# Two pairs of modulation weights move from the GpSimd queue into the weight ring of the SyncE queue

## The chip, the cores and the metric

The kernel runs on one core of a Trainium2 chip (trn2). The metric is the device time of one execution in microseconds (us), as the median of several runs. All data is float32; each large product is made from float32 weights that ScalarE and VectorE split into a high and a low part.

## The reference, cut to what matters

One decoder layer, for 256 prompt tokens and 8 sample tokens together (264 columns). Each of its three blocks begins with an RMS norm that is shifted and scaled by rows of a modulation matrix `mod`, which is itself a product of the conditioning vectors with `w_ada`:

```
mod = silu(c) @ w_ada + b_ada                      # 1024 x 9216, nine rows of 1024
x = x + 0.5 * g1 * SwiGLU_1(rmsnorm(x)*(1+sc1) + sh1)
h = rmsnorm(x)*(1+sc2) + sh2
q, k, v (both branches), gates = h @ w_in          # projections
out_a, out_b = attention over own tokens and paged K/V caches
x = x + g2 * ((sig(gA) * yA + sig(gB) * yB) @ w_out)
x = x + 0.5 * g3 * SwiGLU_2(rmsnorm(x)*(1+sc3) + sh3)
```

## The kernel before

**Stages.** Each engine has one instruction stream, written by hand, and the engines wait for one another on semaphores. In order: a prologue; the first feed-forward block (11 pairs of gate and up weights, then 12 blocks of down weights, `W_DN1` to `W_DN1 + 11`); the projections (`W_QK` to `W_QK + 3` for q, `W_KV` and the seven after it for k and v, then the gates) with the sample tokens' cache blocks scored beside them; attention; the output product; the second feed-forward block.

**The weight ring.** A weight block is 1 MB (or 0.75 MB) and lands in one of four buffers `raw` (`raw_50` to `raw_53` in the listings below are slots 0 to 3). SyncE (SP) issues the loads in the order of `stream_plan`, and `slots` gives each the slot that was filled longest ago. Before a load SP waits in `slot_free` (line 486) until the slot's former content is used up: for a weight block this is its second low half (semaphore `lo_ready`, written by VectorE, DVE), for a pair of modulation weights the product on TensorE (PE) that reads it (semaphore `ada_multiplied`). ScalarE (ACT) copies each half of a landed block to `whi` (`hi`, line 661), DVE subtracts to get `wlo` (`lo`, line 963), PE then runs three products for each chunk (`product`, line 1428). SP works in order, so whatever stands behind a waiting load waits too.

**Modulation weights.** `w_ada` is cut into sets of 2048 columns; a set `sc` has eight 1 MB pieces of 128 rows, which PE reads in four pairs, `ada(sc, q, key_c)` (line 1460). Sets 0 to 2 come through `early` buffers and the ring. Set 3 (`ada(3, 0)` to `ada(3, 3)`, lines 1572 to 1576, after the down blocks and around the sum for the norm) is read from eight `held_ada` buffers, which GpSimd (POOL) loads through its own DMA queue (lines 593 to 598): two when the last gate and up product is done, six when the last activation has been split.

**Around the q projection.** After the last down product: DVE updates `x` (line 1045), ACT squares and takes the root (lines 676, 681), DVE inverts (line 989), then DVE and ACT make the normed input chunk by chunk (lines 998, 700, 1016), on which PE starts `W_QK`. ACT then works through `hi` of `W_QK + 1` (both halves) and `W_QK + 2` (first half) and so on, one block ahead of PE, with the heads' roots (`head_root`, line 683) between; DVE likewise with `lo`, `head_reciprocal` (line 1119) and `head_norm` (line 1123), then it turns the first cache blocks (`turn_keys`, line 1147, L1152 in the rows). SP and POOL each load two cache blocks (`kvA` and `kvB`, eight transfers of 256 KB each) as soon as the last down product is done; POOL loads a third, `kvB_lent`, when the normed input is complete (semaphore `hlo_ready`). SP's `kvA` loads stand behind the loads of `W_QK` to `W_KV` in its order.

A piece of `w_in`, `w_down`, gate or up is fetched in rows of 1 KB (256 columns), a piece of `w_ada` and a cache page in rows of 8 KB.

Of the kernel before, what the change touches and what calls it, by code (L numbers as in the profile page):

```python
# [39 lines left out]
UNIT = 2048  # L40
# [8 lines left out]
W_FF1, W_DN1 = 0, 22  # L49
W_QK, W_KV, W_GATE, W_BR, W_OUT = 34, 38, 46, 54, 58  # L50
# [8 lines left out]
def stream_plan():  # L59
    plan = []  # L60
    ada = lambda c: [("ada", c, 0), ("ada", c, 1)]
    for c in range(ADA_RING):
        plan += ada(c)
    for i in range(NPAIR):
        plan += [("w", W_FF1 + 2 * i)] + (ada(ADA_PRO + i) if i < FF_ADA else []) + [("w", W_FF1 + 2 * i + 1)]
    plan += [("w", W_DN1 + u) for u in range(12)] + [("w", n) for n in range(W_QK, W_DN2 + 12)]
    return plan


# [138 lines left out]
def build(nc, A, O):  # L208
    ctx = ExitStack()
    with ctx:  # L210
# [11 lines left out]
        def sem(name):  # L222
            return ctx.enter_context(nc.semaphore(name))
# [33 lines left out]
        yst = place("yst", [P, 2, D], where=r)  # L257
        ysts = place("ysts", [TS, D], where=r)

        held_at = [hhi_at, hlo_at] + [sil_at + 4 * UNIT * e for e in range(6)]  # L260
        held_ada = [place(f"held_ada{e}", [P, UNIT], where=[o]) for e, o in enumerate(held_at)]

        r = [region]
# [61 lines left out]

        s_raw = [sem(f"raw_landed{s}") for s in range(SLOTS)]
        s_early = [sem(f"early_ada_landed{h}") for h in range(2 * (ADA_PRO - ADA_RING))]
        s_held, s_last = [sem(f"held_ada_landed{e}") for e in range(8)], [sem(f"last_ada_landed{e}") for e in range(4)]
        s_rows, s_crow, s_x, s_const = sem("rows_landed"), sem("crow_landed"), sem("x_landed"), sem("const_landed")
        s_const_late, s_ptab = sem("late_const_landed"), sem("page_table_landed")  # L330
        s_hi, s_lo, s_gemm = sem("hi_ready"), sem("lo_ready"), sem("gemm_done")
# [153 lines left out]
        def _(sp):  # L485
# [52 lines left out]
            sp.wait_ge(s_ptab, 16)  # L538
            for u in range(12):
                load_w(W_DN1 + u)  # L540
            for u in range(4):
                load_w(W_QK + u)
            load_w(W_KV)
            sp.wait_ge(s_gemm, half_done(W_QK - 1, 1))
# [41 lines left out]
        @block.gpsimd  # L586
        def _(pool):
            late = CW["dist"][0]
            pool.dma_start(const[:, 0:late], A["consts"][:, 0:late]).then_inc(s_const, 16)

            pool.wait_ge(s_sil, 1)
            pool.dma_start(const[:, late:NCONST], A["consts"][:, late:NCONST]).then_inc(s_const_late, 16)
            pool.wait_ge(s_gemm, half_done(W_DN1 - 1, 1))
            for e in range(2):
                pool.dma_start(held_ada[e][:, :], ada_src(3, e)).then_inc(s_held[e], 16)
            pool.wait_ge(s_alo, NPAIR)
            for e in range(2, 8):
                pool.dma_start(held_ada[e][:, :], ada_src(3, e)).then_inc(s_held[e], 16)
            pool.wait_ge(s_gemm, half_done(W_QK - 1, 1))
            pool.wait_ge(s_ptab, 16)  # L600
            for use in range(KVS):
                kv_load(pool, 1, use)

            def row_out(name, ab, p, src, srcs, done):
                c0 = 256 * p
                name += ("_moba", "_diff")[ab]
                dst = O[name + "_prompt"][0, 0].rearrange("(a p) h d -> p a (h d)", p=P)[:, :, c0:c0 + 256]
                dsts = O[name + "_sample"][0, :, 0].rearrange("s h d -> s (h d)")[:, c0:c0 + 256]
                f0 = 512 * ab + c0
                pool.dma_start(dst, src[:, :, f0:f0 + 256]).then_inc(done, 16)  # L610
                pool.dma_start(dsts, srcs[:, f0:f0 + 256]).then_inc(done, 16)

            K_ROWS = {6: 0, 10: 1, 12: 2, 14: 3}
            V_ROWS = {7: 0, 15: 1, 17: 2, 19: 3}
            pool.wait_ge(s_ada, ADA_N2 + 4)
            for b in range(2):
                ins = nc.gpsimd.memset(qrow[b][:, :, :], 0.0)
            ins.then_inc(s_qzero, 1)
            def lo(n, t):

                key = ("w", n)
                s = slot_of(key)
                pool.wait_ge(s_raw[s], landed(key))
                pool.wait_ge(s_hi, half_done(n, t))
                pool.wait_ge(s_lo, half_done(n, t) - 1)
                nc.gpsimd.tensor_tensor(half_view(wlo[n % 2], key, t), half_view(raw[s], key, t), half_view(whi[n % 2], key, t).bitcast(F32),  # L626
                                        ALU.subtract).then_inc(s_lo, 1)

            for use in range(KVS, 4 * TS):
                kv_load(pool, 1, use)  # L630
                if use + 2 < POOL_HALVES:
                    lo(*filler(use + 2))
                if use in K_ROWS:
                    i = K_ROWS[use]
                    pool.wait_ge(s_tok, 4 * (i + 1))
                    row_out("k", i // 2, i % 2, ktok, ktoks, s_krow)
                if use in V_ROWS:
                    i = V_ROWS[use]
                    pool.wait_ge(s_vtok, 4 * (i + 1))
                    row_out("v", i // 2, i % 2, vtok, vtoks, s_vrow)  # L640

            def load_last(e):
                pool.dma_start(ada_dst(last_ada[e], ADAS - 1), ada_src(ADAS - 1, e)).then_inc(s_last[e], 16)

            pool.wait_ge(s_pv, 4 * TS)
            load_last(0)
            pool.wait_ge(s_vrow, 16 * 8)
            pool.wait_ge(s_po, KC)
            load_last(1)
            pool.wait_ge(s_ext, 2)  # L650
            load_last(2)
            load_last(3)
# [772 lines left out]
        def _(pe):  # L1425
# [34 lines left out]
            def ada(sc, q, key_c):  # L1460

                b = 4 + sc % 2
                narrow = sc == ADAS - 1
                if q == 0 and sc >= 2:
                    pe.wait_ge(s_adaT, sc - 1)
                for half in range(2):
                    if key_c is None:
                        e = 2 * (q - (ADA_RING if sc == 0 else 0)) + half
                        landing, buf = ((s_early, early) if sc == 0 else (s_last, last_ada) if narrow else (s_held, held_ada))
                        pe.wait_ge(landing[e], 16)  # L1470
                        w = buf[e]
                    else:
                        key = ("ada", key_c, half)
                        s = slot_of(key)
                        pe.wait_ge(s_raw[s], landed(key))
                        w = raw[s]
                    u = 2 * q + half
                    for k in range(2 if narrow else 1):
                        kc = 2 * u + k if narrow else u
                        rows_ = w[:, 1024 * k:1024 * k + 1024] if narrow else w[:, :]  # L1480
                        cols = rows_.rearrange("p (t j a) -> p t j a", j=4, a=32)
                        n = 256 if narrow else 512
                        for j in range(4):
                            ins = mm(bank[32 * j:32 * j + 32, b, 0:n].rearrange("p (t a) -> p t a", a=32), csilu[:, kc, :], cols[:, :, j, :],  # L1484
                                     start=(kc == 0), stop=(kc == KC - 1))
                ins.then_inc(s_ada, 1)
# [63 lines left out]
            def down(first, pairs, alos, xups, with_ada):  # L1550
                for cb in range(4):
                    for third in range(3):
                        n = first + 3 * cb + third
                        if cb == 0:
                            pe.wait_ge(s_alo, alos - NPAIR + (4, 8, 11)[third])
                        if third == 0:
                            if cb == 0:
                                pe.wait_ge(s_sil, pairs)
                            elif cb == 1:
                                pe.wait_ge(s_act, pairs)  # L1560
                            else:
                                pe.wait_ge(s_xup, xups + cb - 1)
                        nk = min(FC - 8 * third, 8)
                        for t in range(2):
                            block_half(2 * (cb % 2), n, n % 2, t, ahi, alo, nk=nk, k0=8 * third, first=(third == 0), last=(third == 2))
                        u = 3 * cb + third
                        if with_ada and cb and third == 1:
                            norm_sum(1, cb - 1)
                        if not with_ada and cb and third == 1:
                            y_turn(cb - 1)  # L1570
                if with_ada:
                    ada(3, 0, None)
                    norm_sum(1, 3)
                    ada(3, 1, None)
                    ada(3, 2, None)
                    ada(3, 3, None)
                else:
                    y_turn(3)

# [345 lines left out]
```

## Time and profile before

| | us |
|---|---|
| median of 3 runs | 784.88 |
| lowest and highest | 783.54 to 786.91 |
| the profiled execution | 784.88 |
| its span in the profile | 783.2 |

Busy shares of the span are PE 93%, DVE 61%, ACT 41%, POOL 16%. The mean DMA rate is 268 GB/s. The profiled execution took 784.88 us, 1.7 us more than the span, and is also the median run, so that a change of the span can be added to the median directly. In the views below a time is counted from the span's start. "SPq" and "POOLq" are the issuing parts of SP and POOL. A group "x3" is three instructions in a row; its length runs from the first start to the last end.

### The profile page before, as it was taken

To read this page: it belongs to the slowest core of one execution; us is meant where nothing else is said; L and a number is where in the kernel's file an instruction comes from. 1 tells how busy PE (TensorE), PEld (TensorE's weight loads), DVE (VectorE), ACT (ScalarE), POOL (GpSimd) and SP (SyncE) were. 2 spreads that over 40 slices of the span, in tenths; PEclk is the share of its full clock that TensorE was granted. 3 is DMA by queue.
4 is the path that set the end of the run, shared out by engine and by line. 5 is a ranking of instruction groups with operands and counts; after the bars stand their busy time and mean duration, and the time that the engine had idled before them with its cause. 6 is when DMAs were issued, how large, how long until landed. Compare 5 with 4: busy or idle time off the path is not lost.

```text
span 783.2 us, 16961 instructions
## 1 busy us (share of the span) xinstructions
PE 730.3 (93%) x6610; PEld 647.7 (83%) x6610; DVE 479.3 (61%) x684; ACT 320.3 (41%) x515; POOL 123.8 (16%) x179
## 2 busy tenths in 40 slices
PE   5589999999999998988878999999989999999997
PEld 2369889999999797877765666669979999999997
DVE  1635454555454899999987554677766465454551
ACT  1434333344242653333314544364445444444331
POOL 0000000002000402877863332210000000000000
PEclk9799999999999999999978999999999999999999
DMA  9979898867986764999999999995625655646530
GB/s 352 381 254 344 291 321 302 269 195 267 395 277 210 273 213 142 388 400 407 405 391 342 404 403 348 342 364 191 199 72 164 205 168 171 204 148 201 165 105 28
DMA packets 116520, 209.53 MB, mean 268 GB/s; under 512 B 6714, under 2 KB 100186, under 8 KB 104162
## 3 DMA queue, kind: packets, MB, share of 16 engines
q1 hardware_dynamic: 106784, 159.47, 59.1%
q0 software_dynamic: 9440, 49.02, 16.0%
q8 instruction: 46, 0.75, 0.4%
q14 instruction: 24, 0.20, 0.1%
q10 hardware_dynamic: 226, 0.10, 0.1%
HBM read 205.31 MB, written 3.24 MB: 266 GB/s over the span
## 4 chain that ended last, share of the span: by engine, by line
PE 70%; DVE 18%; DMA 6%; issue 2%; ACT 2%; SPq 1%; ACTq 0%; DVEq 0%
PE bank L1433 19%; PE bank L1434 19%; PE bank L1435 19%; DMA early<-in_w_ada 3%; PE bank L1789 3%; DVE kvB L1152 2%; DVE kvA L1152 2%; PE bank L1484 2%; DMA kvA<-in_cache_k_moba 2%; DVE rstd L1132 2%; PE bank L1749 1%; DVE wlo L969 1%; DMA raw<-in_w_ada 1%; DVE kvB_lent L1152 1%; PE bank L1750 1%
## 5 line engine op out<-in xcount | busy, mean ns | idle before, releaser
L969 DVE TENSOR_TENSOR wlo<-raw,whi 128x1024 fp32r<-128x1024 f32 (+1 forms) x177 | 208.6, 1199 | 190.3 <-ACT whi L671 187.6
L1433 PE MATMUL bank<-hhi,whi 128*128 128x264 f32 x992 | 288.6, 291 | 11.4 <-DVE wlo L969 7.5
L1434 PE MATMUL bank<-hlo,whi 128*128 128x264 f32 x992 | 283.5, 286 | 0.0
L1435 PE MATMUL bank<-hhi,wlo 128*128 128x264 f32 x992 | 283.1, 285 | 0.0
L671 ACT ACTIVATE whi<-raw 128x1024 fp32r<-128x1024 f32 (+1 forms) x192 | 194.5, 1034 | 119.6 <-PE bank L1435 83.1
L1433 PEld LDWEIGHTS bank<-hhi,whi 128*128 128x128 f32 x992 | 189.3, 191 | 24.6 <-issue 15.1
L1434 PEld LDWEIGHTS bank<-hlo,whi 128*128 128x128 f32 x992 | 189.3, 191 | 0.2
L1435 PEld LDWEIGHTS bank<-hhi,wlo 128*128 128x128 f32 x992 | 188.4, 190 | 0.0
L1433 PE MATMUL bank<-ahi,whi 128*128 128x264 f32 x416 | 119.6, 288 | 0.4 <-DVE alo L1391 0.4
L1435 PE MATMUL bank<-ahi,wlo 128*128 128x264 f32 x416 | 118.1, 284 | 0.0
L1434 PE MATMUL bank<-alo,whi 128*128 128x264 f32 x416 | 117.8, 283 | 0.0
L1433 PEld LDWEIGHTS bank<-ahi,whi 128*128 128x128 f32 x416 | 78.2, 188 | 0.9 <-DVE alo L1391 0.6
L1434 PEld LDWEIGHTS bank<-alo,whi 128*128 128x128 f32 x416 | 78.3, 188 | 0.2
L1435 PEld LDWEIGHTS bank<-ahi,wlo 128*128 128x128 f32 x416 | 78.3, 188 | 0.0
L443 POOL DMA_DIRECT2D kvB<-in_cache_k_diff x44 | 23.2, 528 | 112.1 <-issue 64.8
L706 ACT ACTIVATE sil<-bank 128x528 f32<-128x528 f32 x22 | 13.4, 611 | 62.9 <-PE bank L1435 62.9
L710 ACT ACTIVATE ahi<-act 128x528 f32 (+1 forms) x22 | 14.2, 646 | 54.2 <-DVE act L1023 54.2
L626 POOL TENSOR_TENSOR wlo<-raw,whi 128x1024 fp32r<-128x1024 f32 x15 | 35.9, 2392 | 2.8 <-issue 2.5
L443 POOL DMA_DIRECT2D kvB<-in_cache_v_diff x44 | 23.2, 528 | 51.0 <-PE bank L1789 41.9
L1749 PE MATMUL bank<-hhi,whi 128*128 128x264 f32 x96 | 28.5, 297 | 0.0
L1027 DVE TENSOR_TENSOR alo<-act,ahi 128x528 f32 (+1 forms) x22 | 15.6, 709 | 19.1 <-ACT ahi L710 19.1
L1750 PE MATMUL bank<-hlo,whi 128*128 128x264 f32 x96 | 27.3, 284 | 0.0
(246 smaller groups left out, 804.9 us busy)
## 6 DMA issues: line engine op xcount, KB each, us to landing
raw<-in_ffn_w_gate SPq DMA_DIRECT2D x22, 1024.0 KB, 5.4
raw<-in_ffn_w_up SPq DMA_DIRECT2D x22, 1024.0 KB, 5.4
raw<-in_w_ada SPq DMA_DIRECT2D x20, 1024.0 KB, 8.3
raw<-in_w_in SPq DMA_DIRECT2D x20, 1024.0 KB, 10.5
raw<-in_ffn_w_down SPq DMA_DIRECT2D x16, 1024.0 KB, 5.3
kvB<-in_cache_k_diff POOLq DMA_DIRECT2D x44, 256.0 KB, 6.4
kvA<-in_cache_k_moba SPq DMA_DIRECT2D x44, 256.0 KB, 8.0
kvA<-in_cache_v_moba SPq DMA_DIRECT2D x44, 256.0 KB, 6.3
```

Source lines behind the costliest of these rows:

```text
L443: eng.dma_start(rows_, cache[bass.ds(page, 1)].rearrange("a (j t) d -> (a j) (t d)", t=4)).then_inc(s_kv[ab][use % KVS], 16)
L626: nc.gpsimd.tensor_tensor(half_view(wlo[n % 2], key, t), half_view(raw[s], key, t), half_view(whi[n % 2], key, t).bitcast(F32), ALU.subtra ...
L671: nc.scalar.activation(half_view(whi[key[1] % 2], key, t), half_view(raw[s], key, t), ACT.Copy).then_inc(s_hi, 1)
L969: dve.tensor_tensor(half_view(wlo[key[1] % 2], key, t), half_view(raw[s], key, t), half_view(whi[key[1] % 2], key, t).bitcast(F32), ALU.su ...
L1132: dve.reciprocal(rstd[:, i % 2, :], rstd[:, i % 2, :]).then_inc(s_krecip, 1)
L1152: dve.transpose(slot, slot).then_inc(s_kT[ab], 1)
L1433: mm(out, wh, xh, start=start, stop=False)
L1434: mm(out, wh, xl, start=False, stop=False)
L1435: return mm(out, wl, xh, start=False, stop=stop)
L1749: mm(out, wh, hhi[:, k, :], start=(k == 0), stop=False)
L1750: mm(out, wh, hlo[:, k, :], start=False, stop=False)
L1789: ins = mm(bank[32 * q:32 * q + 32, 4 + ab, :], wpad[half][:, q, ab, w0:w0 + 32], kv_slot(ab, use)[:, q, :], start=(half == 0 and c % 4 == ...
```

## The change

Of set 3 only the first four pieces are still loaded by POOL into `held_ada`. The last two pairs (`ADA_N2 + 2` and `ADA_N2 + 3`, four pieces of 1 MB) go through the ring on SP's queue, between `W_QK` and `W_QK + 1`. `ada(3, 2)` and `ada(3, 3)` read them from there. `W_QK + 1`, `W_QK + 2`, `W_QK + 3` and `W_KV` thereby follow in slots that these pairs hold. POOL's wait for all of set 3 ahead of zeroing `qrow` goes, since the buffers that overlapped it are gone.

```diff
@@ stream_plan
-    plan += [("w", W_DN1 + u) for u in range(12)] + [("w", n) for n in range(W_QK, W_DN2 + 12)]
+    plan += [("w", W_DN1 + u) for u in range(12)] + [("w", W_QK)] + ada(ADA_N2 + 2) + ada(ADA_N2 + 3)
+    plan += [("w", n) for n in range(W_QK + 1, W_DN2 + 12)]
@@ buffers and semaphores
-        held_at = [hhi_at, hlo_at] + [sil_at + 4 * UNIT * e for e in range(6)]
+        held_at = [hhi_at, hlo_at, sil_at, sil_at + 4 * UNIT]
-        s_held, s_last = [sem(f"held_ada_landed{e}") for e in range(8)], [sem(f"last_ada_landed{e}") for e in range(4)]
+        s_held, s_last = [sem(f"held_ada_landed{e}") for e in range(4)], [sem(f"last_ada_landed{e}") for e in range(4)]
@@ sync
             for u in range(12):
                 load_w(W_DN1 + u)
-            for u in range(4):
+            load_w(W_QK)
+            load_pair(ADA_N2 + 2)
+            load_pair(ADA_N2 + 3)
+
+            for u in range(1, 4):
                 load_w(W_QK + u)
             load_w(W_KV)
@@ gpsimd
-            for e in range(2, 8):
+            for e in range(2, 4):
                 pool.dma_start(held_ada[e][:, :], ada_src(3, e)).then_inc(s_held[e], 16)
...
-            pool.wait_ge(s_ada, ADA_N2 + 4)
             for b in range(2):
                 ins = nc.gpsimd.memset(qrow[b][:, :, :], 0.0)
@@ tensor
-                    ada(3, 2, None)
-                    ada(3, 3, None)
+                    ada(3, 2, ADA_N2 + 2)
+                    ada(3, 3, ADA_N2 + 3)
```

SP's order around the end of the first feed-forward block, from its last down block to its first cache page, in the kernel before. The brackets are the semaphores that the instruction waits for.

```order
L508 DMA raw_51<-in_ffn_w_down 128x6x256 [waits lo_ready]
L508 DMA raw_52<-in_w_in 128x8x256 [waits lo_ready]
L508 DMA raw_53<-in_w_in 128x8x256 [waits lo_ready]
L508 DMA raw_50<-in_w_in 128x8x256 [waits lo_ready]
L508 DMA raw_51<-in_w_in 128x8x256 [waits lo_ready]
L508 DMA raw_52<-in_w_in 128x8x256 [waits lo_ready]
L434 TENSOR_LOAD ptab [waits gemm_done]
```

The same place in the changed kernel (its line numbers are one higher).

```order
L509 DMA raw_51<-in_ffn_w_down 128x6x256 [waits lo_ready]
L509 DMA raw_52<-in_w_in 128x8x256 [waits lo_ready]
L503 DMA raw_53<-in_w_ada 128x2048 [waits lo_ready]
L503 DMA raw_50<-in_w_ada 128x2048 [waits lo_ready]
L503 DMA raw_51<-in_w_ada 128x2048 [waits lo_ready]
L503 DMA raw_52<-in_w_ada 128x2048 [waits lo_ready]
L509 DMA raw_53<-in_w_in 128x8x256 [waits ada_multiplied]
L509 DMA raw_50<-in_w_in 128x8x256 [waits ada_multiplied]
L509 DMA raw_51<-in_w_in 128x8x256 [waits ada_multiplied]
L509 DMA raw_52<-in_w_in 128x8x256 [waits ada_multiplied]
L435 TENSOR_LOAD ptab [waits gemm_done]
```

The four `w_in` loads `W_QK + 1` to `W_KV` stood behind waits on DVE's work in the down stage; they now stand behind waits on PE's modulation products, which come after that stage, and everything behind them on SP moves with them.

POOL's order in the kernel before, from the first piece of set 3 on; `held_ada_77` to `held_ada_84` are its eight buffers.

```order
L595 DMA held_ada_77<-in_w_ada 128x2048
L595 DMA held_ada_78<-in_w_ada 128x2048
L598 DMA held_ada_79<-in_w_ada 128x2048
L598 DMA held_ada_80<-in_w_ada 128x2048
L598 DMA held_ada_81<-in_w_ada 128x2048
L598 DMA held_ada_82<-in_w_ada 128x2048
```

Two more pieces follow it. The same place on POOL in the changed kernel, to its first read of the page table.

```order
L600 DMA held_ada_77<-in_w_ada 128x2048
L600 DMA held_ada_78<-in_w_ada 128x2048
L603 DMA held_ada_79<-in_w_ada 128x2048
L603 DMA held_ada_80<-in_w_ada 128x2048
L435 TENSOR_LOAD ptab
```

POOL issues four pieces instead of eight. The orders of PE, ACT and DVE stay as they are.

## Rows read from the trace of the kernel before

**Rows 1.** Chain of waits, 186 to 253 us: shares by line.
```profile
by line: PE bank L1435 32.2%; PE bank L1433 32.0%; PE bank L1434 31.8%; PE bank L1492 4.0%; issue 0.0%
```

**Rows 2.** Chain of waits, 268 to 400 us: start, length, what (us).
```profile
286.14 1.23 DVE wlo L969
287.37 3.38 DVE rstd L1121
...
291.54 2.22 DVE kvA L1152
...
377.90 1.08 PE bank L1678 x32
```

**Rows 3.** VectorE alone: stretch, length, busy time (instructions), clock, DMA share, GB/s.
```profile
266.90:286.10 19.20, 18.55 (x14) 1.00 0.73 241
286.10:377.90 91.80, 89.71 (x90) 1.00 0.86 326
```

**Rows 4.** Timeline, TensorE's modulation products: start, length, line, tile, count.
```profile
44.96 1.92 PE L1484 MATMUL bank<-raw,csilu 128*32 128x512 f32 x16
...
252.89 1.92 PE L1484 MATMUL bank<-held_ada,csilu 128*32 128x512 f32 x16
...
255.99 5.36 PE L1484 MATMUL bank<-held_ada,csilu 128*32 128x512 f32 x48
```

**Rows 5.** Timeline, SyncE's issues, same columns.
```profile
46.94 0.82 SPq L502 DMA_DIRECT2D raw<-in_w_ada  x2
...
49.53 4.01 SPq L513 DMA_DIRECT2D raw<-in_ffn_w_gate  x1
...
227.01 23.58 SPq L508 DMA_DIRECT2D raw<-in_w_in  x5
256.41 5.82 SPq L443 DMA_DIRECT2D kvA<-in_cache_k_moba  x8
272.64 7.06 SPq L508 DMA_DIRECT2D raw<-in_w_in  x2
```

**Rows 6.** Timeline, GpSimd's issues; in brackets the idle time before and its releaser.
```profile
256.35 4.55 POOL L443 DMA_DIRECT2D kvB<-in_cache_k_diff  x8 [64.45 <-issue]
267.20 2.25 POOL L443 DMA_DIRECT2D kvB_lent<-in_cache_k_diff  x4 [6.30 <-DVE hlo L1016]
```

**Rows 7.** L508's two w_in loads issued 243.9 and 250.2: time to landing.
```profile
DMA to landing us min/median/max: 5.0/5.1/5.1
```

**Rows 8.** One line's loads: the w_down load issued at 190.0.
```profile
L508 SPq DMA_DIRECT2D raw<-in_ffn_w_down x1: 368/368/368, 190.0 to 190.0; - x1
...
DMA to landing us min/median/max: 20.9/20.9/20.9
```

**Rows 9.** DMA queues, 189 to 211 us; q0 is GpSimd's, q1 SyncE's.
```profile
q0 software_dynamic: 1107, 8.15, 89.9%
q1 hardware_dynamic: 861, 0.86, 11.3%
```

**Rows 10.** All engines by stretch: the last three figures are clock, DMA share, GB/s.
```profile
190.00:210.00 20.00, 20.00 (x168) 20.00 (x167) 8.20 (x13) 5.20 (x6) 1.89 (x4) 1.00 1.02 411
213.00:227.00 14.00, 14.00 (x115) 13.87 (x113) 8.55 (x11) 6.46 (x8) 0.00 (x0) 1.00 1.10 348
```

**Rows 11.** DMA traffic, 258 to 273 us.
```profile
DMA packets 947, 5.15 MB, mean 343 GB/s; under 512 B 320, under 2 KB 320, under 8 KB 320
```

**Rows 12.** Timeline of ScalarE around the q projection.
```profile
265.86 2.94 ACT L671 ACTIVATE whi<-raw 128x1024 fp32r<-128x1024 f32 x3
...
271.61 1.06 ACT L671 ACTIVATE whi<-raw 128x1024 fp32r<-128x1024 f32 x1 [0.88 <-PE bank L1435]
```

**Rows 13.** Timeline of VectorE around the q projection.
```profile
272.78 1.22 DVE L969 TENSOR_TENSOR wlo<-raw,whi 128x1024 fp32r<-128x1024 f32 x1 [0.17 <-ACT whi L671]
273.92 3.44 DVE L1121 RECIPROCAL rstd<-rstd 128x528 f32<-128x528 f32 x1
```

**Rows 14.** Waits, 180 to 255 us: who waited for whom; total, times, longest.
```profile
ACT whi L671 <- DMA raw<-in_ffn_w_down: 3.8, 2, 2.8
```

## The prediction, made before the changed kernel had run

> **What bounds the kernel now.** I read the chain of waits first, then the stages around the changed loads, then the queues.
>
> In the down stage the chain runs through TensorE alone, nearly all of it weight products [rows 1]: no load and no other engine sets the time there. From 286 us to 378 us it runs through VectorE: low halves, head norms, turning of cache blocks, and it goes back to TensorE only at 377.9 [rows 2]. VectorE alone shows how full it is: 89.7 of 91.8 us, and already 18.55 of 19.2 us in the stretch before, 266.9 to 286.1 [rows 3]. So TensorE's 93% doesn't say what a delay in the q projection is worth. VectorE has 0.65 us to spare from 267 to 286 and what it loses beyond that is paid to the end, because everything it does afterwards stands in its fixed order.
>
> **What goes.** POOL's eight pieces become four. In the stretch in which they are in flight POOL's queue moves 8.15 MB and SP's 0.86 MB [rows 9], and a down block issued then lands after 20.9 us [rows 8]. That will get better by about 4 MB, some 10 us of DMA time at 411 GB/s [rows 10]. It is worth nothing: the chain in that stage has no load and no VectorE row in it [rows 1], so TensorE's work hides it. For POOL's removed wait I take nothing too: TensorE ends set 3 at 261.35 (255.99 + 5.36) [rows 4], and POOL zeroes `qrow` only behind the issue of kvB_lent at 267.2 to 269.45 [rows 6], so the wait was over long before.
>
> **What the new pieces need.** SP now issues them where it issued `W_QK + 1` to `W_KV`, the last at about 250.2, and such a load lands 5.1 us later [rows 5, 7]: 255.3. TensorE reads the last piece in the last eighth of a group that ends at 261.35, about 260.7. Five microseconds to spare: nothing.
>
> **What is moved.** The loads of `W_QK + 1`, `+ 2`, `+ 3` and `W_KV` wait for `ada(3, 2)` (the first two) and `ada(3, 3)`. The group of 48 products is three such steps of 1.79 us, so `ada(3, 2)` ends at 259.6 and `ada(3, 3)` at 261.35 [rows 4]. How fast SP follows is seen early in the kernel: products end at 46.88 (44.96 + 1.92), the next pair's load is issued at 46.94 [rows 4, 5]. So `W_QK + 1` is issued at 259.7 instead of some 233. The question is whether it and the next two still land when they are needed.
>
> Need: ScalarE starts on `W_QK + 1` at 265.86, and on the first half of `W_QK + 3` at 271.61 [rows 12]. VectorE makes that half's low part at 272.78 and then begins the first head reciprocal at 273.92 [rows 13].
>
> Supply. Back to back, 1 KB rows move at 348 GB/s, 8 KB rows at 411 [rows 10]: 1.05 MB takes 3.0 us and 2.55 us. An undisturbed load lands after 5.1 us [rows 7], so about 2.1 us of it is not transfer. When POOL's queue has 8 KB rows in flight, SP's 1 KB rows get 0.86 of 9.01 MB, a tenth [rows 9]. And POOL does have such rows in flight: kvB's 2.1 MB from 256.35 on, kvB_lent's 1.05 MB from 267.2 on [rows 6]. Before, the loads beside them were kvA's, with rows of 8 KB too, and nothing was late.
> - kvB: bytes from 256.35 + 2.1 = 258.45, 5.1 us at 411 GB/s, over at 263.5.
> - `W_QK + 1`: bytes from 259.7 + 2.1 = 261.8; a tenth of the rate until 263.5 (0.07 MB), then 0.98 MB in 2.8 us: 266.3. That is 0.45 us after 265.86.
> - `W_QK + 2`: 3.0 us more, 269.3.
> - kvB_lent: bytes from 269.3 on, 2.6 us to 271.9. `W_QK + 3` gets 0.1 MB in that time, the other 0.95 MB need 2.7 us: 274.6. `W_KV`: 277.6.
>
> So ScalarE can start on `W_QK + 3` at 274.6; its copy takes 1.06 us and VectorE's step 1.22 us [rows 12, 13], with 0.1 us between: VectorE is at the reciprocal at 277.0 instead of 273.92, **3.1 us late**. Of its 0.65 us of spare time [rows 3] about half lies behind this point, 0.3 us. 2.8 us remain. TensorE itself is hardly held: `W_QK + 1` starts some 0.5 us later, and `W_QK + 3` is due there only at about 282. The delay goes through VectorE to the reciprocals and cache blocks of the chain [rows 2].
>
> kvA moves too. SP's last `w_in` issue may be held until the queue drains (such an issue took 4.0 us with three loads in front [rows 5]), so to about 266; then the page table (kvA's first issue at 256.41 came 3.5 us after the end of the down stage at 252.9), then 5.8 us for eight issues [rows 4, 5]: `W_KV + 1` is issued at 275.3 instead of 272.64. Bytes in order: `W_KV` until 277.6, kvA 5.1 us until 282.7, `W_KV + 1` until 285.7. Its low half was made at 286.14 [rows 2], now at 288.9, so it has to land by 287.8: 2.1 us to spare. kvA is first turned at 291.54 [rows 2]; 282.7 is early enough.
>
> Sum: -0 (POOL's burst) + 0 (new pieces) + 2.8 (VectorE through `W_QK + 3`) + 0 (kvA, `W_KV + 1`). Against the profiled execution: span 783.2 + 2.8 = 786.0, plus the 1.7 us outside it, **787.7**; the profiled execution is the median.
>
> **Bounds.** Lower: if SP's queue were served as though alone, three loads from 261.8 end at 270.8, before 271.61: nothing lost, 784.9. Below nothing I see no term, since no wait on the chain goes. Upper: all bytes of POOL first and the mixed rate of 343 GB/s [rows 11]: 3.15 MB of weights, 0.7 MB of kvB left at 261.8, 1.05 MB of kvB_lent, 4.9 MB in 14.3 us: 276.1, 4.5 us late, 4.2 after the spare time: 789.1. I take 2.8, from the shares of rows 9 and the full rates of rows 10, as they are for the same two row sizes.
>
> **A rule beside the rows.** [Rows 8] show a 1 MB load that took 20.9 us. The Trainium skill, DMA: Bandwidth & Descriptors, section "Anatomy of one DMA — SWDGE (gpsimd) path", fits a transfer as 2.0 us plus bytes over 436 GB/s. By that alone, an estimate, `W_QK + 1` would land at 259.7 + 4.4 = 264.1, the third load at about 269, and nothing would be late (784.9, the first rival's result). The same page, section "Queues, rings and completion order", has each DMA engine take turns between queues packet by packet, without regard to bytes; rows 9, with 8.15 against 0.86 MB at rows of 8 against 1 KB, agree with turns by count.
>
> **The rivals.**
> - *The loads come in time* (784.9). The condition: kvB and kvB_lent take less from SP's queue than a tenth-to-nine-tenths split, or end sooner, so that `W_QK + 3` has landed by 272. For: kvB is only 2 MB where rows 9 had 8, and POOL issues it in pieces of 256 KB that may leave gaps (the mean rate there was 343, not 411 GB/s [rows 11]). Against: the bytes have to pass in any order, and 4.9 MB take 11.9 us even at 411 GB/s, so not before 273.7 unless kvB_lent falls behind.
> - *A second load is late as well* (slower). The issue of `W_QK + 3` and `W_KV` is held longer than 4 us and takes the page table, kvA and `W_KV + 1` with it; POOL's next transfers share with them. From a landing of 287.8 on each microsecond counts. For: behind a queue slowed to a tenth an issue should be held longer than 4.0 us. Against: there are 2.1 us to spare, and what waits in the queue is transferred meanwhile. If the held issue takes twice as long and ends at 270, `W_KV + 1` is issued at 279.3 and lands at about 290: 2.2 us more, 789.9.
> - *The freed burst is worth something* (faster). ScalarE does wait 3.8 us for down blocks in that stage [rows 14]; if TensorE waited with it, all of that would come back: 784.9 - 3.8 = 781.1. Against it, [rows 1] have no such wait in the chain, TensorE being a block behind.
>
> **How the numbers follow.** Forecast (1 to 4.2 us lost): 0.57. In time: 0.2. Second load late: 0.18. Faster: 0.03; the rest is what I don't see. The time is the forecast's, 787.7. The range goes from 784.0 (in time, with the spread of the runs before) to 790.5 (the second load late). A measurement of this kernel can tell about 0.5%, 3.9 us, from no change: faster than 781.0 is 0.04; slower than 788.8 takes most of the second rival and the upper end of the forecast, 0.26; within, 0.70.
>
> **What would show it.** Right, step by step: no change of TensorE's time up to 252.9; `w_in` loads issued at about 259.7, 260.1, 261.4; landings after 6.6 us and then about 9 and 13 us instead of 5.1; a wait of ScalarE on a `w_in` load of some 2 us shortly before 275, and VectorE's first wide reciprocal near 277; the chain from there on as before, about 3 us later, up to the end. Wrong: a first reciprocal still at 274 (the loads came in time), a VectorE wait before 289 on `W_KV + 1` (second rival), a down stage that ends before 252.5, or a delay at 290 that has gone by 400.

## The result: 5.6 us slower, and where they went

The changed kernel takes **790.42 us** (median of 7 runs, 788.2 to 792.2), the kernel before 784.78 us (783.39 to 786.91, 7 runs beside them). The ratio is 1.0076, 95% interval 1.0053 to 1.0097. The ratios here and below are not the quotients of the printed medians, from which they differ by up to 0.002. The forecast was 787.7: slower, by half of what was measured.

The page of the profile of the changed kernel (span 789.4 us) answers to the shares given in the section on the time before. Total busy times have hardly moved (TensorE 733.2 us after, 730.3 before in the page); what was added is waiting.

```profile
span 789.4 us, 16961 instructions
PE 733.2 (93%) x6610; PEld 651.9 (83%) x6610; DVE 480.1 (61%) x684; ACT 320.8 (41%) x515; POOL 121.6 (15%) x175
```

The two profiled executions differ by 1.1 us before the change can matter (the prologue). I therefore count from VectorE's update of `x` at the end of the down stage, 253.00 us in the kernel before, 251.90 in the changed one; this point is called the mark below. First the timeline of the issues, SyncE's and then GpSimd's (start, length, count), to be held against [rows 5, 6].

```profile
232.20 17.24 SPq L503 DMA_DIRECT2D raw<-in_w_ada  x4
258.58 9.77 SPq L509 DMA_DIRECT2D raw<-in_w_in  x4
271.83 6.65 SPq L444 DMA_DIRECT2D kvA<-in_cache_k_moba  x8
278.52 6.37 SPq L509 DMA_DIRECT2D raw<-in_w_in  x2
...
255.24 4.55 POOL L444 DMA_DIRECT2D kvB<-in_cache_k_diff  x8 [66.53 <-issue]
266.09 2.25 POOL L444 DMA_DIRECT2D kvB_lent<-in_cache_k_diff  x4 [6.30 <-DVE hlo L1020]
```

`W_QK + 1` is issued at 258.58, 6.7 us after the mark, where the forecast put it (259.7 less 253.0). Now ScalarE and VectorE in the timeline of the changed kernel, to be held against [rows 12, 13]. The brackets are idle time and its releaser.

```profile
268.33 2.00 ACT L675 ACTIVATE whi<-raw 128x1024 fp32r<-128x1024 f32 x2 [3.48 <-DMA raw<-in_w_in]
272.57 1.06 ACT L675 ACTIVATE whi<-raw 128x1024 fp32r<-128x1024 f32 x1 [2.24 <-DMA raw<-in_w_in]
276.80 1.06 ACT L675 ACTIVATE whi<-raw 128x1024 fp32r<-128x1024 f32 x1 [1.23 <-DMA raw<-in_w_in]
...
269.49 1.23 DVE L973 TENSOR_TENSOR wlo<-raw,whi 128x1024 fp32r<-128x1024 f32 x1 [4.05 <-ACT whi L675]
277.96 1.23 DVE L973 TENSOR_TENSOR wlo<-raw,whi 128x1024 fp32r<-128x1024 f32 x1 [1.06 <-ACT whi L675]
279.11 3.45 DVE L1125 RECIPROCAL rstd<-rstd 128x528 f32<-128x528 f32 x1
285.65 3.45 DVE L1125 RECIPROCAL rstd<-rstd 128x528 f32<-128x528 f32 x1
```

ScalarE waits for three loads in a row: it stood ready for 3.5, 2.2 and 1.2 us when they landed. The first wide reciprocal stands 27.2 us after the mark; before it was 20.9 (273.92 less 253.00). That is 6.3 us, and the second one is 6.15 us late. The chain of waits of the changed kernel shows the same hand-over. It runs through the first late load, then TensorE, and from 290 on through VectorE as in [rows 2], each step some 6.2 us later after the mark.

```profile
253.10 0.65 ACT work L680
258.58 9.73 DMA raw<-in_w_in
268.33 1.07 ACT whi L675
269.49 1.24 DVE wlo L973
...
290.03 1.07 ACT whi L675
291.19 1.23 DVE wlo L973
292.42 3.37 DVE rstd L1125
295.81 0.77 DVE qT L1131
296.58 2.22 DVE kvA L1156
```

### The profile page after: what moved, and what is told of

The parts are those of the page before. It is cut to its first block, busy times and chain, and to the rows that moved or that the text cites. A ratio compares the mean times of both kernels' runs of the same rounds, so it can differ in the third digit from the quotient of the medians.

```text
span 789.4 us, 16961 instructions
## 1 busy us (share of the span) xinstructions
PE 733.2 (93%) x6610; PEld 651.9 (83%) x6610; DVE 480.1 (61%) x684; ACT 320.8 (41%) x515; POOL 121.6 (15%) x175
## 4 chain that ended last, share of the span: by engine, by line
PE 72%; DVE 13%; DMA 9%; issue 2%; ACT 2%; SPq 1%; ACTq 0%; DVEq 0%
PE bank L1437 19%; PE bank L1438 19%; PE bank L1439 19%; DMA early<-in_w_ada 3%; PE bank L1793 3%; PE bank L1488 2%; DMA kvA<-in_cache_k_moba 2%; DMA kvA_lent<-in_cache_k_moba 2%; DVE kvA L1156 2%; DVE kvB L1156 1%; PE bank L1753 1%; DMA raw<-in_w_in 1%; PE bank L1682 1%; DVE wlo L973 1%; PE bank L1754 1%
## 5 line engine op out<-in xcount | busy, mean ns | idle before, releaser
L710 ACT ACTIVATE sil<-bank 128x528 f32<-128x528 f32 x22 | 13.4, 611 | 61.6 <-PE bank L1439 61.6
L1754 PE MATMUL bank<-hlo,whi 128*128 128x264 f32 x96 | 27.2, 284 | 0.0
```

The costliest lines, as they stand in the source:

```text
L1754: mm(out, wh, hlo[:, k, :], start=False, stop=False)
```

## The experiments

For each run two positions on VectorE after the mark are given beside the time, read from the one profiled execution: the first wide reciprocal, and the second turned block of `kvA` (at 307.50 in the kernel before, 54.50 after the mark), by which the delay that is kept can be read. Kernels that differ only elsewhere agree in them within 0.1 us, where times scatter by 3. All ratios are to runs of the kernel before beside them.

| kernel | first reciprocal after the mark | against before | second `kvA` block against before | ratio of times (95%) |
|---|---|---|---|---|
| before | 20.92 | | | |
| changed | 27.21 | +6.29 | +6.16 | 1.0076 (1.0053 to 1.0097) |
| x1_wait_only | 27.65 | +6.73 | +6.39 | 1.0056 (1.0035 to 1.0077) |
| x2_kvb_later | 20.96 | +0.04 | +5.61 | 1.0080 (1.0053 to 1.0107) |
| x3_one_pair | 20.94 | +0.02 | +0.02 | 0.9989 (0.9969 to 1.0008) |
| x4_filler | 26.79 | +5.87 | +5.39 | 1.0083 (1.0053 to 1.0113) |
| x5_burst_spread | 20.92 | 0.00 | 0.00 | 0.9986 (0.9963 to 1.0009) |
| x6_kvb_after_kv1 | 20.91 | -0.01 | +1.34 | 1.0016 (0.9995 to 1.0038) |
| x7_lent_after_kv1 | 25.31 | +4.39 | +4.40 | 1.0061 (1.0038 to 1.0084) |
| x8_lent_filler | 23.91 | +2.99 | +2.57 | 1.0059 (1.0032 to 1.0087) |
| v1_pool_lo | 20.91 | -0.01 | -1.11 | 0.9970 (0.9946 to 0.9994) |
| v1_again | 20.91 | -0.01 | -1.11 | 0.9980 (0.9961 to 0.9999) |

The position of the `kvA` block is the one to hold against the times: on 785 us the ratios say 6.0 us for the changed kernel, 6.3 for x2 and 1.3 for x6. It differs from the first reciprocal's where a delay or a gain enters behind the reciprocal (x2, x6, v1) or where a delay is partly made up (x1, x4, x8). It lies within the ratio's interval in each run but x1, where it is 0.3 us above.

### x1_wait_only: the late issue alone, on the kernel before

```diff
-            for u in range(4):
-                load_w(W_QK + u)
+            load_w(W_QK)
+            sp.wait_ge(s_ada, ADA_N2 + 3)
+            load_w(W_QK + 1)
+            load_w(W_QK + 2)
+            sp.wait_ge(s_ada, ADA_N2 + 4)
+            load_w(W_QK + 3)
             load_w(W_KV)
```

> The kernel before with one thing from the change: SP waits for ada(3, 2) ahead of the load of W_QK + 1, and for ada(3, 3) ahead of W_QK + 3. The pieces of set 3 stay where they were, all eight on POOL's queue. Theory (the late issue of these loads is the whole loss): 788.5 to 792 us, like the changed kernel's 790.4, and VectorE's first wide reciprocal 5 to 6.5 us later than in the kernel before. Rival (the loss comes from reading or loading the pairs through the ring, or from POOL's shorter queue): below 786.5.

Measured: 790.86 us (787.67 to 792.91), reciprocal 6.7 us late, a little beyond the 6.5 expected. Two waits on SyncE make the whole loss without a single piece of set 3 in the ring. So the pairs in the ring and POOL's shorter queue are not needed for the loss. The timeline of VectorE, with the waits behind late copies:

```profile
270.04 1.23 DVE L973 TENSOR_TENSOR wlo<-raw,whi 128x1024 fp32r<-128x1024 f32 x1 [4.35 <-ACT whi L675]
275.53 1.23 DVE L973 TENSOR_TENSOR wlo<-raw,whi 128x1024 fp32r<-128x1024 f32 x1 [2.16 <-ACT whi L675]
279.79 3.45 DVE L1125 RECIPROCAL rstd<-rstd 128x528 f32<-128x528 f32 x1
```

### x3_one_pair: half the change

```diff
-    ... [("w", n) for n in range(W_QK, W_DN2 + 12)]
+    ... [("w", W_QK)] + ada(ADA_N2 + 3)
+    plan += [("w", n) for n in range(W_QK + 1, W_DN2 + 12)]
-            for e in range(2, 8):
+            for e in range(2, 6):
-                    ada(3, 3, None)
+                    ada(3, 3, ADA_N2 + 3)
```

(`held_at` and `s_held` get six entries, SP loads the one pair behind `W_QK`, POOL keeps its wait.)

> Half the change: only the last pair of set 3 goes through the ring, the other six pieces stay with POOL. By the slots W_QK + 1 and W_QK + 2 then keep their early issue (about 239 and 250), only W_QK + 3 and W_KV wait for ada(3, 3), to about 260 or 261. Theory (lateness of W_QK + 1 to + 3 against their use): W_QK + 3 lands 268 to 271, before it is needed at about 271.6, time 784 to 786. Rival (each piece in the ring costs, the dose halves the effect): 787 to 788.

Measured: 784.31 us (783.01 to 787.74), beside 785.19 of the kernel before; reciprocal in place. Half the dose costs nothing. `W_QK + 3` is issued at 260.5, as late as in the change, and lands after 7.4 us, at 267.9, before it is needed: `W_QK + 1` and `+ 2` are no longer in flight ahead of it. This is lateness against a use, not a cost per piece.

### x2_kvb_later: POOL silent beside the first three loads

```diff
             pool.wait_ge(s_ptab, 16)
+            pool.wait_ge(s_raw[slot_of(("w", W_QK + 3))], landed(("w", W_QK + 3)))
             for use in range(KVS):
                 kv_load(pool, 1, use)
```

> The changed kernel, but POOL issues its first three cache blocks only when W_QK + 3 has landed, so nothing of POOL's queue is in flight beside W_QK + 1 to W_QK + 3. Theory A (the loads lose their time to POOL's 8 KB rows): W_QK + 1 lands about 7 us after its issue as in the early pair issued at 46.94 (instead of 9.7), W_QK + 3 some 5 us earlier than in the changed kernel, time 785.5 to 787.5. Theory B (the issue at 259 is too late whatever stands beside it): W_QK + 3 earlier by less than 2 us, time 789 to 791. Both expect the first wide reciprocal to move with the landing of W_QK + 3.

Measured: 791.11 us (788.49 to 795.89), and the reciprocal back in its place. The loads issued at 258.6, 259.1 and 260.4 landed after 5.2, 7.8 and 9.6 us, in the changed kernel after 9.7, 13.5 and 16.5. So theory A holds for the landings, and B is out: issued as late as in the change, they come in time when POOL is silent. Yet nothing was won. A's range for the time was missed by 3.6 us, and the time lies at the upper edge of B's, whose mechanism is out. The timeline of VectorE and the landing of `W_KV + 1` in this kernel say why.

```profile
290.70 1.23 DVE L974 TENSOR_TENSOR wlo<-raw,whi 128x1024 fp32r<-128x1024 f32 x1 [5.71 <-ACT whi L676]
...
L509 SPq DMA_DIRECT2D raw<-in_w_in x1: 584/584/584, 272.7 to 272.7; - x1
...
DMA to landing us min/median/max: 16.8/16.8/16.8
```

kvB, now issued at 273.37, lies beside the next load that VectorE needs, and that one takes 16.8 us. The delay was moved from `W_QK + 3` to `W_KV + 1`: 5.6 us at the second `kvA` block. The first reciprocal alone would not have shown it.

### x6_kvb_after_kv1: POOL silent two loads longer

The same wait as in x2, on `("w", W_KV + 1)` instead of `("w", W_QK + 3)`.

> The changed kernel, but POOL issues its first three cache blocks only when W_KV + 1 has landed, two loads later than in x2_kvb_later. Theory A, amended (1 KB loads starve beside POOL's 8 KB rows wherever POOL is put, and in x2 it was W_KV + 1, landed after 16.8 us, that took over from W_QK + 3): W_KV + 1 lands by 281, the low half that stood at 286.14 stays within 1 us, kvB lands before its use at about 293, time 784.5 to 786.5. Rival (the change costs in some other way that x2 and the changed kernel share, the loads being a symptom): 789 to 791.

Measured: 786.99 us (785.03 to 788.96), 0.5 us above the expected range; ratio 1.0016, about 1.3 us, not told apart from none (by the medians it is 2.5). `W_KV + 1` landed after 9.3 us, at 282.7, and the low half that stood at 286.14 is in its place. In the trace the changed issue order with POOL's transfers out of the way loses 1.3 us instead of 6.2; by the times at least half of the loss is gone. What is left is seen in the timeline of VectorE: it waits 1.24 us for kvB, which now comes too late itself.

```profile
273.36 3.45 DVE L1126 RECIPROCAL rstd<-rstd 128x528 f32<-128x528 f32 x1
...
294.43 2.31 DVE L1157 STREAM_TRANSPOSE kvB<-kvB 128x2048 f32<-128x2048 f32 x1 [1.24 <-DMA kvB<-in_cache_k_diff]
```

### x7_lent_after_kv1: only the third cache block held back

```diff
             for use in range(KVS):
+                if use == KVS - 1:
+                    pool.wait_ge(s_raw[slot_of(("w", W_KV + 1))], landed(("w", W_KV + 1)))
                 kv_load(pool, 1, use)
```

> The changed kernel with only the third cache block (kvB_lent) held back until W_KV + 1 has landed; the first two as in the change. Theory A: kvB still makes W_QK + 1 and W_QK + 2 late, kvB_lent no longer W_QK + 3, which lands about 3 us earlier than in the changed kernel; first wide reciprocal about 3 us earlier, time 786.5 to 788.5. Rival (kvB alone makes all the delay, through the first landing): 789.5 to 791.

Measured: 790.72 us (787.73 to 794.12), reciprocal 4.4 us late instead of 6.3. The third load landed 13.4 us after its issue (16.5 in the change), 3.1 us earlier, as expected, but only 1.9 us arrived at the reciprocal. So with kvB alone beside the loads 4.4 us of delay are left. The expected 3 us at the reciprocal and the range of the time were missed; the time lies in the rival's range, though the trace doesn't bear the rival out, since 1.9 us did go. Something else stood right behind the landing. In the timeline of x7 VectorE waits for ScalarE's fourth copy, and that copy for TensorE:

```profile
276.01 1.06 ACT L677 ACTIVATE whi<-raw 128x1024 fp32r<-128x1024 f32 x1 [1.30 <-PE bank L1441]
277.17 1.23 DVE L975 TENSOR_TENSOR wlo<-raw,whi 128x1024 fp32r<-128x1024 f32 x1 [1.14 <-ACT whi L677]
278.31 3.45 DVE L1127 RECIPROCAL rstd<-rstd 128x528 f32<-128x528 f32 x1
```

### x4_filler and x8_lent_filler: TensorE's clock

In the changed kernel TensorE idles 4.38 us for `W_QK + 1`'s low half, and then its granted clock is at half (1.2 of 2.4 GHz). By stretch, with the clock as the third figure from the right:

```profile
265.00:269.50 4.50, 1.48 (x12) 1.27 (x11) 0.45 (x2) 1.17 (x2) 3.22 (x6) 1.00 1.09 352
269.70:276.50 6.80, 5.64 (x25) 5.67 (x26) 5.13 (x6) 3.64 (x5) 0.50 (x1) 0.50 1.06 375
```

Both kernels add work to TensorE in that idle time, x4 to the changed kernel and x8 to x7:

```diff
                     pe.wait_ge(s_xup, 4)
+                if u == 1:
+                    for c in range(KC):
+                        mm(bank[:, 7, 0:T], C("ones"), x[:, c, :], start=(c == 0), stop=(c == KC - 1))
```

> The changed kernel with eight added products on TensorE (ones by x into bank 7, not used for anything) between W_QK and W_QK + 1, about 3.6 us of work in TensorE's new idle time of 4 us. Theory C (part of the loss is TensorE's half clock from 269.7 to 276.5, which follows that idle time): no such stretch, W_QK + 1's products in 3 us a half instead of 6, and 2 to 3 us gained at the end: 787.5 to 788.5. Theory D (VectorE, behind the landing of W_QK + 3, sets the delay and TensorE's clock there is hidden): the clock stays up, but the reciprocal and the time stay, 789.5 to 791.

> x7_lent_after_kv1 with the eight added products of x4_filler on TensorE between W_QK and W_QK + 1. In x7 the landing of W_QK + 3 no longer held ScalarE; it waited 1.3 us for TensorE instead, whose clock had dropped to 1.2 GHz at 271.9 to 275.3. Theory (two delays lie side by side: the landings, and TensorE's clock after its idle time; with the first reduced the second sets the time): no such stretch and a first wide reciprocal 0.8 to 1.5 us earlier than in x7, time 0.5 to 1.5 us below x7. Rival (the clock is hidden here too, as in x4): the reciprocal within 0.3 us of x7's.

Measured: x4 791.43 us (789.96 to 794.05), reciprocal 26.79 after the mark, 0.4 us earlier than in the change. x8 790.26 us (785.43 to 792.95), reciprocal at 23.91, 1.4 us earlier than in x7. In both the low clock of 270 to 276 is gone. So both delays existed side by side. In x4 the landing of `W_QK + 3` is the later one, and ScalarE still waits for it; its own 0.4 us earlier landing is the whole 0.4 us at the reciprocal (theory D, and the time is 0.4 us above D's range). In x7 that landing is 21.8 after the mark and TensorE comes 1.2 us behind it; in x8 the landing is at 21.6 and sets the reciprocal again. Further on the clock counts for more: at the second `kvA` block x4 is 0.8 us ahead of the change and x8 1.8 us ahead of x7. In the times neither can be told: x8 is 0.5 us below x7, inside the scatter of both. From here, x8's timeline of VectorE:

```profile
276.02 2.38 DVE L975 TENSOR_TENSOR wlo<-raw,whi 128x1024 fp32r<-128x1024 f32 x2 [0.50 <-ACT whi L677]
278.32 3.45 DVE L1127 RECIPROCAL rstd<-rstd 128x528 f32<-128x528 f32 x1
```

(its mark is at 254.41, so 278.32 is 23.91 after it).

### x5_burst_spread: the shorter burst alone, on the kernel before

```diff
             for e in range(2, 8):
+                if e == 4:
+                    pool.wait_ge(s_gemm, half_done(W_DN1 + 5, 1))
                 pool.dma_start(held_ada[e][:, :], ada_src(3, e)).then_inc(s_held[e], 16)
```

> The kernel before, with POOL's burst halved alone: the last four pieces of set 3 are issued only after the sixth down block, everything else unchanged. If the shorter burst is worth something by itself, 781 to 783.5; if TensorE hides it, as the forecast has it, within 1 us of the kernel before (784 to 786). Down blocks at 190 to 213 should land earlier by several microseconds either way.

Measured: 784.96 us (782.87 to 788.76), ratio 0.9986 with 1 in the interval. The landings of the down blocks issued from 190 to 212, in x5 and then before:

```profile
L508 SPq DMA_DIRECT2D raw<-in_ffn_w_down x5: 367/368/368, 190.0 to 210.0; - x5
DMA to landing us min/median/max: 5.4/8.8/13.1
...
L508 SPq DMA_DIRECT2D raw<-in_ffn_w_down x4: 368/3142/6446, 190.0 to 206.4; - x4
DMA to landing us min/median/max: 14.8/19.7/21.8
```

A median 11 us better, and no time won: TensorE hid it, as forecast.

### v1_pool_lo and v1_again: three low halves on POOL

The low halves that stand at 286.14, 295.87 and 302.85 on VectorE in the kernel before go to POOL, which idles from 271 to 307. Nothing else is changed in the kernel before.

```diff
@@ gpsimd, ahead of its loop over the cache blocks
+            for k in range(2, 5):
+                lo(*filler(k))
             for use in range(KVS, 4 * TS):
@@ vector
-                lo(W_QK + u + 2, 0)
+                if u < 3:
+                    lo(W_QK + u + 2, 0)
...
-            lo(*filler(3))
...
-            lo(*filler(4))
```

> A version against the kernel before, from the reading that VectorE sets the time from 267 to 378: three low halves (first of W_KV + 1, second of W_KV + 1, first of W_KV + 2) are made by POOL, which is idle there, instead of VectorE. If VectorE's load is the bound, it saves 3 x 1.14 = 3.4 us there less what POOL's slower step (2.4 us) makes TensorE wait: 781.5 to 783.5. If TensorE's order takes over at once or POOL slows VectorE, 784 to 787.

> v1_pool_lo once more, beside other runs of the kernel before: if its ratio of 0.997 was more than the scatter of this kernel, it is again between 0.994 and 0.999; if it was scatter, 0.998 to 1.002.

Measured: 783.72 us (780.87 to 786.52) and 783.47 us (781.36 to 786.79), one just outside and one at the upper end of the expected range; ratios 0.9970 and 0.9980, each interval just below 1. It is a small gain, 1.6 to 2.4 us by the ratios, 0.8 and 1.3 by the medians, 1.1 in both traces, and below the 3.4 us that VectorE saves. The timelines of POOL and VectorE show where the rest goes: VectorE, full before, now waits 3.2 us for TensorE's product with q (L1665). That product is not held by POOL's slower step (2.38 us against VectorE's 1.2): TensorE waits for no low half between 285 and 300 and runs its own products without a gap from 293 on. So TensorE's order takes over.

```profile
292.59 2.38 POOL L626 TENSOR_TENSOR wlo<-raw,whi 128x1024 fp32r<-128x1024 f32 x1 [5.98 <-ACT whi L673]
...
300.72 0.42 DVE L1253 COPY qrep<-bank 128x256 f32<-128x256 f32 x1 [3.21 <-PE bank L1665]
```

## Why the prediction was right in kind and half in size

**Right.** POOL's shorter burst is worth nothing (x5), the new pieces land in time (no wait of TensorE for them, and x1 loses as much without them), SyncE follows TensorE's products within 0.1 us, the delay enters through the landing of `W_QK + 3` at VectorE and is then kept (6.3 us at the first reciprocal, 6.15 at the second and third). The first rival, loads in time, is out: all three were late, and the landing after 4.4 us, which the prediction set beside the rows by a rule for the GpSimd path, took 9.7 us.

The second rival is half true. Its condition came about: the last two `w_in` issues were held 4.5 and 3.5 us, SyncE was free 16.5 us after the mark (forecast 13, rival 17), and `W_KV + 1` was issued at 26.6 and landed at 35.7 (forecast 22.3 and 32.7, rival 26.3 and about 37). It cost nothing only because the larger delay stood before it: its copy waited for TensorE until 290.03, the load had landed at 287.6. With the forecast's 2.8 us it would have been due at 34.8 and 0.9 us late. x2 shows this term at full size, with kvB beside that load.

**Wrong: the term of 2.8 us (VectorE through `W_QK + 3`), which measured 6.15.** The step that failed is the supply of the three loads. Its parts, after the mark:

| | forecast | measured | off by |
|---|---|---|---|
| `W_QK + 1` issued | 6.7 | 6.7 | 0 |
| `W_QK + 1` landed | 13.3 | 16.4 | 3.1 |
| `W_QK + 2` landed | 16.3 | 20.6 | 4.3 |
| `W_QK + 3` landed | 21.6 | 24.9 | 3.3 |
| first wide reciprocal | 24.0 | 27.2 | 3.2 |

Two of my lines failed. One is "5.1 us at 411 GB/s" for kvB. The other is the placing of all 2.1 us that are not transfer ahead of the bytes, which makes a load land with its last byte. The DMA traffic of the changed kernel, first from 257 to 261 where POOL's queue is alone, then from the first load's issue to its landing, 258.6 to 268.3:

```profile
DMA packets 196, 1.11 MB, mean 277 GB/s; under 512 B 61, under 2 KB 61, under 8 KB 61
q0 software_dynamic: 196, 1.11, 89.1%
...
DMA packets 2074, 3.28 MB, mean 338 GB/s; under 512 B 115, under 2 KB 1897, under 8 KB 1897
q1 hardware_dynamic: 1801, 1.82, 56.9%
q0 software_dynamic: 272, 1.44, 43.1%
```

kvB, fetched in pieces of 256 KB to 32 partitions each, moves at 277 GB/s in the 4 us in which it is alone, not at the 411 of [rows 10], most of which were full pieces of `w_ada`; it therefore lies in the way longer. Why it moves more slowly no run shows. And when `W_QK + 1` (1.05 MB) lands, 1.82 MB of SyncE's queue have passed, 0.77 MB of them of later loads. With POOL silent, in x2, the same load landed when 1.34 MB had passed:

```profile
DMA packets 1328, 1.34 MB, mean 254 GB/s; under 512 B 16, under 2 KB 1328, under 8 KB 1328
q1 hardware_dynamic: 1328, 1.34, 77.3%
```

The same count for all three loads, from stretches of the DMA view that end there: when SyncE's queue had moved the bytes of one, two and three loads, and when the load landed.

| | x2: bytes, landing | changed: bytes, landing |
|---|---|---|
| `W_QK + 1` | 263.1, 263.8 | 266.1, 268.3 |
| `W_QK + 2` | 266.1, 266.8 | 269.1, 272.6 |
| `W_QK + 3` | 269.1, 269.9 | 274.7, 276.8 |

With POOL silent a load lands 0.7 to 0.8 us after its bytes, beside POOL's rows 2.1 to 3.4 us. So a competing queue not only takes rate, it also makes loads issued close together land later than their bytes say. By bytes the third load is 1.2 us later than forecast; the landing 2.1 us after that is the larger part of the miss. The share of a tenth did not hold either: from 270 to 274, beside kvB_lent, SyncE's queue moved 0.51 MB and POOL's 1.05. That cost the forecast little, since all of these bytes have to pass. That some of the sixteen DMA engines had more of POOL's pieces than others would explain the late landings; the profile doesn't name the engines, and the cause stays open. The Trainium skill says in DMA: Bandwidth & Descriptors, section "Issuing engines are not separate DMA queues", that transfers of all issuing engines interleave on the same 16 DMA engines; x2 against the changed kernel agrees, 5.2 against 9.7 us for the same load.

TensorE's new idle time and half clock are a term that the sum did not have: it let `W_QK + 1` start "some 0.5 us later", and TensorE stood idle for 4.4. In the change itself this was hidden at the first reciprocal and worth 0.8 us further on (x4). With a landing 3.1 us earlier, in x7, it set the reciprocal: 4.4 us against x8's 3.0 with the clock up. Whether TensorE's clock would have fallen too with landings as early as I forecast, no run shows.

**The rest of the time.** The profiled pair differs by 6.2 us over the span and by 7.3 from the mark to the end, 1.1 more than the delay at the reciprocals. Followed on VectorE, the changed kernel is 6.2 us late up to 312 us, 9.0 at 350 and 7.3 at 460 and from there to the end. x5, whose time equals that of before, is 0.0 late at 312, 3.0 at 350 and 0.1 at 460. So the 3 us that come in between 312 and 350 are not of the change; x5 makes all of them up, the changed kernel 1.7. They go with TensorE's clock: in x5 it was at half for 3.4 us between 302 and 312 and again between 335 and 345, in the changed kernel between 308 and 318 and between 340 and 350, and in the profiled execution of before in none of these stretches. The same stretch, x5 and then before:

```profile
302.00:312.00 10.00, 8.15 (x128) 7.35 (x128) 9.15 (x15) 2.62 (x6) 2.57 (x5) 0.83 0.33 97
...
302.00:312.00 10.00, 7.94 (x160) 6.75 (x160) 9.09 (x15) 4.13 (x10) 4.04 (x5) 1.00 0.41 123
```

Such stretches come and go between executions, and times differ with them. v1_pool_lo and v1_again are the same kernel, with spans of 780.2 and 785.1 us: 3.2 us of the difference lie ahead of the mark, where the mean clock from 25 to 50 us was 0.86 and 0.73, and 1.7 behind it, with 0.77 and 0.66 from 515 to 530. That the clock makes the whole scatter is not shown. What stays open is whether x7 and x8, with 4.4 and 2.6 us at the second `kvA` block, cost as much in time as their medians say (6.2 and 5.5 us over the runs beside them); their intervals, 3.0 to 6.6 and 2.5 to 6.8 us, contain the delay seen in the trace, x8's only just.

## What to carry to other kernels

When a load is moved later, cost it by what is in flight on the other queues at its new place. Here loads in 1 KB rows beside another queue's 8 KB rows landed 9.7 to 16.5 us after their issue instead of 5.2 to 9.6. Take its landing from a row with the same neighbours, not from an undisturbed one, and allow for a landing well after the last byte. A fix that moves the competing transfer has to be followed to the next load beside which it comes to lie; look for that at the next wait of the full engine, not at the one that was mended. And an engine at 61% of the span can be the one that is full for 90 us: a delay of 6.2 us there was paid in full, and three steps moved off it (3.4 us) were won only as far as the next engine let them (1.1 us in the trace).

## What the runs showed of the hardware that was not expected

- With the same issue order on SyncE, POOL's 8 KB rows beside SyncE's 1 KB rows turned a landing of 5.2 us into 9.7 and one of 9.6 into 16.5 (x2 against the change), and one of 9.3 into 16.8 (x6 against x2, for `W_KV + 1`).
- SyncE's loads landed 0.7 to 0.8 us after their share of the queue's bytes had passed when POOL's queue was silent (x2), and 2.1 to 3.4 us after it beside POOL's transfers (the change).
- Transfers of 256 KB from POOL's queue, alone from 257 to 261 us in the change, moved at 277 GB/s; eight of 1 MB in the kernel before, with a tenth of SyncE's bytes among them, at 411.
- After 4.4 us of idle time TensorE's granted clock was 0.50 for 6.8 us; with eight otherwise unused products in that gap it was 1.00 (x4 from 262 to 278 us, x8 from 268 to 280).
